# Expert weights loaded as runs of 16 KB per partition, with the contracted rows renumbered to match

## What is computed

```python
logits = t @ w_router + b_router              # t: normed rows (280, 1024); 32 experts
top_v, top_i = lax.top_k(logits, 4)           # four experts for each row
gates = softmax(top_v)
def expert_block(xb, ei):
    gu = xb @ w_gate_up[ei] + b_gate_up[ei]   # (1024, 2048) of each expert
    gate = minimum(gu[:, :1024], 7.0)
    up = clip(gu[:, 1024:], -7.0, 7.0)
    act = gate * sigmoid(gate * 1.702)
    return ((up + 1.0) * act) @ w_down[ei] + b_down[ei]   # (1024, 1024)
y = segment_sum(yp[dest] * g_s, tok_s)        # weighted sum back onto the rows
```

## Time and profile before

| | us |
|---|---|
| median of 3 runs | 1342.67 (1340.54 to 1344.32) |
| the profiled execution | 1343.27 |
| its span, first to last instruction | 1341.4 |
| mean granted clock of TensorE in it | 0.973 of full speed |

### The profile page before, as it was taken

One profiled execution on the slowest core, in us unless ns is written; L12 is line 12 of the kernel. 1 busy time (PEld: TensorE's weight loads), 2 busy tenths in 40 slices (PEclk: granted clock), 3 DMA queues, 4 the chain that ended last, 5 costly groups with the idle time before them and its releaser, 6 DMA issues.

```text
span 1341.4 us, 15435 instructions
## 1 busy us (share of the span) xinstructions
PE 1260.1 (94%) x6339; PEld 606.3 (45%) x6339; DVE 315.5 (24%) x591; ACT 159.9 (12%) x305; POOL 84.5 (6%) x110
## 2 busy tenths in 40 slices
PE   5999999999799999999999999999999999999986
PEld 4757666764533434343443434343443434343431
DVE  2334446442211111122111111121111111121112
ACT  2214322112100001010000001010000001010001
POOL 4176500000000000000000000000000000000000
PEclk9989999989599999999999999999999999999998
DMA  9247570345386999999999999999999999999991
GB/s 316 79 131 245 170 250 1 139 196 184 157 322 260 414 421 414 419 417 417 419 414 422 414 422 414 419 417 417 419 415 422 414 422 414 419 417 417 420 414 43
DMA packets 92203, 447.63 MB, mean 334 GB/s; under 512 B 6282, under 2 KB 15926, under 8 KB 59269
## 3 DMA queue, kind: packets, MB, share of 16 engines
q1 hardware_dynamic: 85495, 427.36, 79.2%
q0 software_dynamic: 5632, 18.88, 4.5%
q10 hardware_dynamic: 1046, 0.97, 0.3%
HBM read 445.74 MB, written 1.68 MB: 334 GB/s over the span
## 4 chain that ended last, share of the span: by engine, by line
PE 76%; DMA 17%; DVE 3%; ACT 2%; issue 1%; SPq 1%; ACTq 0%; DVEq 0%
PE ps L942 19%; PE ps L997 17%; DMA arena<-in_w_gate_up 16%; PE ps L900 11%; PE ps L776 5%; PE ps L749 2%; PE ps L1009 2%; PE ps L605 2%; DVE arena L1642 2%; PE ps L1018 1%; PE ps L492 1%; PE ps L623 1%; PE ps L1014 1%; PE ps L538 1%; PE ps L646 1%
## 5 line engine op out<-in xcount | busy, mean ns | idle before, releaser
L942 PE MATMUL ps<-arena 128*64 128x512 f32 x2048 | 452.5, 597 | 30.8 <-DMA arena<-in_w_gate_up 23.6
L942 PEld LDWEIGHTS ps<-arena 128*64 128x64 f32 x2048 | 155.9, 137 | 315.2 <-issue 314.8
L997 PE MATMUL ps<-arena 128*64 128x512 f32 x1024 | 225.2, 597 | 4.8 <-ACT arena L1043 4.8
L1043 ACT ACTIVATE arena<-ps 128x512 f32<-128x512 f32 (+9 forms) x170 | 96.0, 582 | 532.2 <-PE ps L997 210.8
L900 PE MATMUL ps<-arena 128*128 128x128 f32 (+1 forms) x768 | 142.7, 318 | 1.3 <-DVE arena L1601 1.3
L997 PEld LDWEIGHTS ps<-arena 128*64 128x64 f32 x1024 | 74.4, 138 | 145.1 <-issue 144.6
L900 PEld LDWEIGHTS ps<-arena 128*128 128x128 f32 (+1 forms) x768 | 109.0, 195 | 44.2 <-issue 15.5
L1622 DVE TENSOR_SCALAR arena<-ps 128x512 f32<-128x512 f32 x32 | 22.1, 691 | 420.2 <-PE ps L942 420.2
L1217 ACT ACTIVATE arena<-arena 128x512 f32<-128x512 f32 x32 | 20.2, 630 | 490.1 <-DVE arena L1622 490.1
L1639 DVE TENSOR_TENSOR arena<-arena,ps 64x512 f32<-64x512 f32 x16 | 10.9, 679 | 270.0 <-PE ps L1014 270.0
L776 PE MATMUL ps<-arena 128*128 128x280 f32 x256 | 66.0, 414 | 0.0
(11 more groups left out here) (286 smaller groups left out, 765.9 us busy)
## 6 DMA issues: line engine op xcount, KB each, us to landing
arena<-in_w_gate_up SPq DMA_DIRECT2D x128, 2048.0 KB, 15.5
arena<-in_w_down SPq DMA_DIRECT2D x64, 2048.0 KB, 16.9
arena<-in_w_in SPq DMA_DIRECT2D x8, 1024.0 KB, 9.4
arena<-in_w_out SPq DMA_DIRECT2D x2, 2048.0 KB, 11.7
arena<-in_w_in SPq DMA_DIRECT2D x2, 1088.0 KB, 12.9
arena<-in_w_in SPq DMA_DIRECT2D x1, 2048.0 KB, 23.5
arena<-in_consts SPq DMA_DIRECT2D x1, 1104.0 KB, 8.8
arena<-in_w_uq SPq DMA_DIRECT2D x1, 768.0 KB, 15.8
```

The source lines that it names most:

```text
L942: m = mm(ps[SL * e:SL * e + SL, b, :], xg[:, 2 * c + kk, SL * e:SL * e + SL], w[e][:, kk, b, :], start=(c == 0 and kk == 0), stop=(c == 3 ...
L997: m = mm(ps[SL * e:SL * e + SL, u, :], hidT[:, 4 * c + kk, SL * e:SL * e + SL], w[e][:, kk, u, :], start=(c == 0 and kk == 0), stop=(c == ...
L1043: return act.activation(out, in_, ACT.Copy)
```

## The change

The rows of each weight matrix are dealt to the partitions in another order. A partition's rows for one chunk now follow each other in memory: two rows of `w_gate_up` or four rows of `w_down`, 16 KB either way. In `w_gate_up` partition p has rows 8p to 8p+7, and quarter c takes rows 8p+2c and 8p+2c+1; the runs of neighbouring partitions are 64 KB apart. In `w_down` half c takes rows 512c+4p to 512c+4p+3; the runs of neighbouring partitions touch. The order of chunks, their sizes, the slots and all waits stay as they are.

As a sum over rows doesn't depend on their order, the left operands are renumbered to match. `h2` is written with its columns permuted (L1530): the engine walks the row in natural order and writes with a step of 128 numbers. `w_rt` is loaded in the same order, eight rows of 128 B for each partition in one run of 1 KB. `hid` is written with a permutation of its own (L1631), again with a step of 128; this can't be done in place, so `hid` now lies over `gate`, and `ye` over `up`.

```diff
-        hid, ye = up, gate
+        hid, ye = gate, up
...
-        gu_rows = a["w_gate_up"].rearrange("l e (k p) n -> p (l e k) n", p=P)
-        dn_rows = a["w_down"].rearrange("l e (k p) n -> p (l e k) n", p=P)
+
+        gu_rows = a["w_gate_up"].rearrange("l e (p c k) n -> p (l e) c (k n)", p=P, k=2)
+        dn_rows = a["w_down"].rearrange("l e (c p k) n -> p (l e) c (k n)", p=P, k=4)
...
-            sp.dma_start(w_rt, a["w_router"][0].rearrange("(k p) e -> p k e", p=P)).then_inc(in_router, 16)
+            sp.dma_start(w_rt, a["w_router"][0].rearrange("(p k) e -> p k e", p=P)).then_inc(in_router, 16)
...
             def load(p, c, dst, signal):
-                rows, k, count = (gu_rows, 2 * (c // 2), 2) if c < 8 else (dn_rows, 4 * (c // 2 - 4), 4)
-                sp.dma_start(dst.rearrange("p (k n) -> p k n", k=count),
-                             rows[:, bass.ds((2 * p + c % 2) * KD + k, count), :]).then_inc(signal, 16)
+                rows, k = (gu_rows, c // 2) if c < 8 else (dn_rows, c // 2 - 4)
+                sp.dma_start(dst.unsqueeze(1), rows[:, bass.ds(2 * p + c % 2, 1), k, :]).then_inc(signal, 16)
...
-                dve.scalar_tensor_tensor(out=h2[0:n, t, :], in0=x[0:n, t, :], scalar=small[0:n, 16 + t:17 + t],
-                                         in1=norm2_g[0:n, :], op0=ALU.mult, op1=ALU.mult).then_inc(h2_ready, 1)
+
+                natural = [v.rearrange("p (q k) -> p q k", k=KD) for v in (x[0:n, t, :], norm2_g[0:n, :])]
+                dve.scalar_tensor_tensor(out=h2[0:n, t, :].rearrange("p (k q) -> p q k", k=KD), in0=natural[0],
+                                         scalar=small[0:n, 16 + t:17 + t], in1=natural[1], op0=ALU.mult, op1=ALU.mult
+                                         ).then_inc(h2_ready, 1)
...
-                    dve.tensor_tensor(hid[:, at_u], up[:, at_u], sgm[:, at_u], ALU.mult).then_inc(hid_ready, 1)
+
+                    natural = [v[:, at_u].rearrange("p (q k) -> p q k", k=4) for v in (up, sgm)]
+                    dve.tensor_tensor(hid[:, at_u].rearrange("p (k q) -> p q k", k=4), *natural, ALU.mult
+                                      ).then_inc(hid_ready, 1)
```

## The result

The changed kernel takes 1324.19 us (median of 4 runs, 1321.42 to 1325.19) against 1342.72 (4 runs): a ratio of 0.9876, with a 95% interval of 0.9852 to 0.9900. The forecast was 1321 in a range of 1315 to 1336. The profiled execution took 1325.19, its span 1323.4. All of the gain and a little more lies where it was looked for, in the stream of weights: 13 pairs took 19.5 us less, while the spans of the two profiled executions differ by 18.0. The changed kernel came 0.9 us later to these pairs and took 0.6 us longer behind them. One execution among all that follow, the profiled one of e4_same_rows_4kb, took 4350 us and is left out of every time.

The account below looks back on a forecast made before the run. The prediction took the stream of weights as the bound, with TensorE's pace close behind. It summed 1343.27 - 21.5 + 1.1 + 0.4 - 1.7 = 1321.6 us, the median 0.6 lower: 1321, in a range of 1315 to 1336.

Parts of the forecast that it names:

- The bound: In the expert pairs the stream of weights sets the pace, 60.24 us a pair; TensorE's own 58.33 is next.
- Part 1: Weight loads: 16 KB runs save 1.52 us a pair, 60.24 to 58.72; gain 21.5 us in all.
- the faster stream never runs dry: Weight stream: slots coming free only as TensorE goes on would not hold up the faster stream; costed at nothing.
- Part 2: `h2` written with a step (L1530): 0.7 us more for 1024 numbers, +1.1 us on the path, between 0 and 2.8.
- Part 3: `hid` written with a step (L1631): +0.35 us an instruction, hidden except in the last pair, +0.4 us there.
- Part 4: Last pair's c = 3: a shorter wait keeps the granted clock at 1.00; -1.7 us, between -1.7 and 0.
- (a): Only `w_down` gains, runs over 8 KB being cut or dearer for a KB; about 1334 us; chance 0.11.
- (b): The 64 KB step of `w_gate_up` between neighbouring partitions slows its loads; chance of a loss over 4 us 0.10.
- (c): Weight loads: run size doesn't matter, no change, 1343 or 1344 us; chance 0.07 together with a mild (b).

Follow-up runs that it names:

- e4_same_rows_4kb: Changed kernel with every row in the same place but each 16 KB run moved as four 4 KB runs in two transfers; median 1364.20 us.
- e1: Changed kernel with only `w_down` in 16 KB runs and `hid` permuted; load of `w_gate_up`, `w_rt` and `h2` as before; median 1329.34 us.
- e2: Changed kernel with only `w_gate_up` in 16 KB runs, `h2` and the router permuted; `w_down` and `hid` as before; median 1333.0 us.
- e9: Changed kernel, rows in the same place, runs cut to the old sizes (8 KB `w_gate_up`, 4 KB `w_down`) in two transfers a chunk; median 1341.82 us.
- e10: Changed kernel, but from pair 2 on only half of each chunk of `w_down` is loaded; median 1313.74 us.
- e8: Changed kernel with `h2` and `hid` written in plain order, so VectorE has no step at all; median 1320.03 us.

## Why the prediction was right, and where it was off

**The bound and Part 1.** Right, by its own steps. The line through 1, 4 and 8 KB gave 611.9 ns for a run of 16 KB. DMA view of the changed kernel, 945 to 975 us:

```profile
DMA packets 882, 12.85 MB, mean 428 GB/s; under 512 B 98, under 2 KB 98, under 8 KB 98
```

784 runs in 30 us are 30 x 16 / 784 = 612.2 ns. A pair of 58.72 was forecast and 58.74 measured; 0.91 of the gain was to come from `w_down` and 0.61 from `w_gate_up`, and e1 and e2 show 0.91 and 0.60. e9 shows that the number of runs sets the rate, and e10 that TensorE's own 58.2 us a pair lies right under it.

**That the faster stream never runs dry** was costed at nothing and is not quite so. Windows of the changed kernel and of before, 476 to 480 us, at the end of pair 1, where TensorE still sets the pace:

```profile
476.00:480.00 4.00, 4.00 (x21) 1.23 (x17) 0.00 (x0) 0.60 (x1) 0.00 (x0) 1.00 0.96 371
```

```profile
476.00:480.00 4.00, 4.00 (x16) 1.27 (x12) 0.00 (x0) 0.60 (x1) 0.00 (x0) 1.00 1.02 424
```

At 371 instead of 428 GB/s the stream loses about 0.5 us there, once. Slots come free no sooner than before, so a faster stream has less in hand; but the engines' share is still 0.96, so the rows show the loss and not its cause. Over the whole of 436 to 508 us the stream moves at 422 GB/s (417 before), so about 0.9 us was gained there and not 1.8. From then on it stays at 428.

**Part 2.** The estimate from L1426, 0.7 us for 1024 numbers, came out as 1.98 - 1.28 = 0.70. On the path to the gathering it is 1.4 us against 1.1 in the sum (e8), and at c = 3 of pair 2 nothing of it is left, which the sum didn't have. c = 3 of pair 2 was to start at 506.95 - 1.8 + 1.1 = 506.3 and started at 507.9, 1.6 later. 0.9 of that is none of the change's doing: L840 already starts at 305.82 instead of 304.91, and TensorE's L482, near the start of the span, at 15.09 instead of 14.26. Another 0.9 is what the stream didn't gain from 436 to 508. The two make up the difference only if the step costs its 1.1 there; with the nothing that e8 shows, about 0.9 us stays unexplained.

**Part 3.** 1056 - 692 = 0.36 us an instruction, against 0.35. Only the last pair shows it: L965 waits 1.8 us instead of 1.5 for L1631, now L1636.

**Part 4 failed.** The wait of the last pair did shrink, to 0.59 us, and its c = 3 did run at 7.09 us. But the granted clock fell a little later. Timeline of the changed kernel, last pair:

```profile
1271.53 7.09 PE L942 MATMUL ps<-arena 128*64 128x512 f32 x32 [0.59 <-DMA arena<-in_w_gate_up]
...
1281.87 1.11 PE L965 MATMUL ps<-arena 128*128 128x128 f32 x4 [1.81 <-DVE arena L1636]
1282.92 9.61 PE L997 MATMUL ps<-arena 128*64 128x512 f32 x32
```

and its window in the middle of that L997:

```profile
1283.00:1287.00 4.00, 4.00 (x10) 1.16 (x12) 0.69 (x1) 0.00 (x0) 0.00 (x0) 0.50 1.00 426
```

Half the full clock for these 4 us, and this L997 takes 9.61 us. In the kernel before it took 7.02, but a later one was slow there, which the prediction left out: the chain that ended last, and a window in it.

```profile
1302.47 7.02 PE ps L997 x32
...
1314.09 8.71 PE ps L997 x32
```

```profile
1314.00:1318.00 4.00, 4.00 (x14) 1.24 (x14) 0.00 (x0) 0.00 (x0) 0.00 (x0) 0.57 0.00 0
```

From the start of c = 3 to the end of the span it is 1323.4 - 1271.53 = 51.9 us against 1341.4 - 1290.12 = 51.3 before; the sum had 51.3 - 1.7 + 0.4 = 50.0. That term, -1.7 for a clock that was to stay up, came out near zero, and is the largest single miss: 1.9 us. With the 1.6 at pair 2 and 0.2 over the 13 pairs it makes up, to 0.1, the 3.6 between 1321.6 and the profiled 1325.19.

The step that failed is the premise that the clock goes by the length of the wait for weights, down after 2.16 us and not after 1.7. e9 waits 2.95 us before its last c = 3 and runs it at 7.09; it also has the same 1.81 us wait for VectorE as the changed kernel, and L997 (L1005 there) runs at 7.09 behind it:

```profile
1292.92 7.09 PE L950 MATMUL ps<-arena 128*64 128x512 f32 x32 [2.95 <-DMA arena<-in_w_gate_up]
...
1303.26 0.66 PE L973 MATMUL ps<-arena 128*128 128x128 f32 x4 [1.81 <-DVE arena L1644]
1303.85 7.09 PE L1005 MATMUL ps<-arena 128*64 128x512 f32 x32
```

What decides where the clock falls in the last pair was not tried. In the profiled executions of e2 and e9 only one group of 32 matmuls in that stretch is slow (8.78 us, the later L997), and c = 3 to the end takes 49.4 and 49.9 us; in the others it takes 51.0 to 51.9.

**The rivals.** (a), runs over 8 KB cut or dearer for a KB: no, 16 KB packets move at the line's rate. (b), the 64 KB step: no, from 16 KB to 2 MB the pairs are the same. (c), size without effect: no, e9.

## What to carry to other kernels

Where transfers fill the DMA engines, read the cost of one run from two or three stretches that have one size each, time x 16 / packets, and draw the line: here some 9.5 ns for a run and 37.65 ns for a KB, from 1 to 16 KB. A sum over rows lets you deal the rows to the partitions so that runs grow, if the left operand is renumbered where it is cheap to do so. Then look how far the next bound is: here 2 us a pair, of which the change took 1.5.

## What was not expected of the hardware

Neighbouring partitions whose runs lie 2 MB apart are loaded as fast as those whose runs touch, 428 GB/s in both. A step costs VectorE 0.36 us for 512 numbers when it is in the write (1056 ns) and 0.40 when it is in the two reads (1091), against 692 without. And a delay ahead of a stretch at the lower granted clock need not reach the end: 1.4 us at the first gathering were 0.5 us one quarter of a pair later. The granted clock did not follow the length of the wait before a group: it fell after 2.16 us in the kernel before and not after 2.95 in e9.
